# Four of the sixteen low halves of each two-stream norm move from VectorE to GpSimd

## What is computed

```python
def rms_norm(x, g):
    xf = x.astype(jnp.float32)
    y = xf * lax.rsqrt(jnp.mean(xf * xf, axis=-1, keepdims=True) + RMS_EPS)
    return (y * g.astype(jnp.float32)).astype(x.dtype)

def modulate(h, shift, scale):
    return h * (1.0 + scale) + shift

def sandwich_ffn(x, w_gate_up, w_down, g_pre, g_post, shift, scale, gate):
    h = modulate(rms_norm(x, g_pre), shift, scale)
    return x + 0.5 * gate * rms_norm(swiglu(h, w_gate_up, w_down), g_post)
...
    for l in range(DEPTH):
        last = l == DEPTH - 1
        mx = [m[:, None, :] for m in mod_vectors(c, w_mod[l], b_mod[l])]
        mc = mod_vectors(c_ctx, w_mod[l], b_mod[l])
```

## Time and profile before

| | before |
|---|---|
| median of 3 runs | 3280.05 us (3278.34 to 3292.75) |
| profiled execution, own time | 3276.89 us |
| its span | 3274.9 us |
| PE busy | 3064.8 us, 94% |
| DVE busy | 1678.6 us, 51% |
| ACT busy | 1354.5 us, 41% |
| POOL busy | 213.9 us, 7% |
| granted TensorE clock, mean | 0.960 of full speed |

### The profile page before, as it was taken

One profiled execution on the slowest core, in us unless ns is written; L12 is line 12 of the kernel. 1 busy time (PEld: TensorE's weight loads), 2 busy tenths in 40 slices (PEclk: granted clock), 3 DMA queues, 4 the chain that ended last, 5 costly groups with the idle time before them and its releaser, 6 DMA issues. The chain is left out here.

```text
span 3274.9 us, 52918 instructions
## 1 busy us (share of the span) xinstructions
PE 3064.8 (94%) x21712; PEld 2694.9 (82%) x21712; DVE 1678.6 (51%) x2574; ACT 1354.5 (41%) x2092; POOL 213.9 (7%) x304
## 2 busy tenths in 40 slices
PE   6999989989999899997989899998999999988998
PEld 4777858657777688876789889998799989988998
DVE  3332254552322633235655557656675677556765
ACT  3222232632222432223455455546464555454644
POOL 1111014101110000011200000000000000000000
PEclk9999989989999899998989999999899999989999
DMA  8555344135554223253245543554265546543553
GB/s 275 167 179 171 99 133 124 40 104 179 177 167 145 90 90 102 91 163 117 67 146 191 167 154 112 185 168 137 65 193 193 160 146 202 191 141 104 168 193 104
DMA packets 405772, 474.85 MB, mean 145 GB/s; under 512 B 10860, under 2 KB 383164, under 8 KB 405578
## 3 DMA queue, kind: packets, MB, share of 16 engines
q1 hardware_dynamic: 380176, 389.05, 36.9%
q0 software_dynamic: 24544, 82.74, 8.0%
q10 hardware_dynamic: 858, 0.29, 0.0%
HBM read 470.84 MB, written 4.84 MB: 145 GB/s over the span
## 5 line engine op out<-in xcount | busy, mean ns | idle before, releaser
L425 DVE TENSOR_TENSOR w_lo<-w_raw,w_hi 128x1024 fp32r<-128x1024 f32 x734 | 897.3, 1228 | 1268.8 <-ACT w_hi L422 1267.7
L433 PE MATMUL bank<-a_hi,w_hi 128*128 128x256 f32 (+1 forms) x3864 | 1241.3, 321 | 57.8 <-DVE a_lo L1398 16.6
L434 PE MATMUL bank<-a_lo,w_hi 128*128 128x256 f32 (+1 forms) x3864 | 1227.1, 318 | 0.0
L435 PE MATMUL bank<-a_hi,w_lo 128*128 128x256 f32 (+1 forms) x3864 | 1226.3, 317 | 0.0
L422 ACT ACTIVATE w_hi<-w_raw 128x1024 fp32r<-128x1024 f32 x734 | 771.1, 1056 | 987.5 <-PE bank L435 957.1
L433 PEld LDWEIGHTS bank<-a_hi,w_hi 128*128 128x128 f32 x3864 | 741.2, 192 | 134.5 <-issue 76.0
L435 PEld LDWEIGHTS bank<-a_hi,w_lo 128*128 128x128 f32 x3864 | 741.5, 192 | 50.5
L434 PEld LDWEIGHTS bank<-a_lo,w_hi 128*128 128x128 f32 x3864 | 741.4, 192 | 47.7
L433 PE MATMUL bank<-h_hi,w_hi 128*128 128x256 f32 (+1 forms) x1728 | 544.5, 315 | 0.0
L435 PE MATMUL bank<-h_hi,w_lo 128*128 128x256 f32 (+1 forms) x1728 | 539.6, 312 | 0.0
L434 PE MATMUL bank<-h_lo,w_hi 128*128 128x256 f32 (+1 forms) x1728 | 539.5, 312 | 0.0
(11 more groups left out here) (289 smaller groups left out, 2320.7 us busy)
## 6 DMA issues: line engine op xcount, KB each, us to landing
w_raw<-in_mlp_w SPq DMA_DIRECT2D x128, 1024.0 KB, 5.3
w_raw<-in_w_ffn_gate_up SPq DMA_DIRECT2D x88, 1024.0 KB, 5.3
m_raw<-in_w_mod POOLq DMA_DIRECT2D x128, 512.0 KB, 4.8
w_raw<-in_w_ffn_down SPq DMA_DIRECT2D x32, 1024.0 KB, 5.9
w_raw<-in_gla_w_in SPq DMA_DIRECT2D x24, 1024.0 KB, 5.5
w_raw<-in_w_in SPq DMA_DIRECT2D x16, 1024.0 KB, 6.0
w_raw<-in_ple_w_gate SPq DMA_DIRECT2D x16, 1024.0 KB, 5.1
w_raw<-in_w_ffn_down SPq DMA_DIRECT2D x16, 768.0 KB, 6.2
```

The source lines that it names most:

```text
L425: e.tensor_tensor(lo, raw, hi.bitcast(F32), ALU.subtract).then_inc(S.lo_ready.sem, 1)
L433: e.matmul(dst, hi, rhs_hi, start=start, stop=False)
L434: e.matmul(dst, hi, rhs_lo, start=False, stop=False)
L435: return e.matmul(dst, lo, rhs_hi, start=False, stop=stop)
```

## The change

In the five norms over both streams, piece 1 of every four (1, 5, 9 and 13 of 16: stream 1 of k0, k2, k4 and k6) gets its `a_lo` from GpSimd. DVE has one operation for it; GpSimd has two: it adds the shift (a column, broadcast) to `z` in place, and subtracts `a_hi` into `a_lo`. TensorE waits for GpSimd's count as well ahead of these blocks. `a_shared` stays as it is until the next norm, so that later products with a `ready` list wait for a count long reached.

```diff
@@ slot_products
                         if k0 + k in ready:
                             e.wait_ge(ready[k0 + k][0].sem, ready[k0 + k][1])
+                        if k0 + k in at.a_shared:
+                            e.wait_ge(S.pool.sem, at.a_shared[k0 + k])
@@ pre_norm
-                scaled, done = {}, {}
+                scaled, done, at.a_shared = {}, {}, {}
...
                     if j >= lag:
                         k, s, c = tiles[j - lag]
+                        if n == TT and (j - lag) % 4 == 1:
+                            if pool:
+                                e.wait_ge(S.act.sem, scaled[j - lag])
+                                e.tensor_tensor(z[:, k, c], z[:, k, c], shift[:, k, s:s + 1].to_broadcast([P, T]), ALU.add).then_inc(S.pool.sem, 1)
+                                e.wait_ge(S.pool.sem, S.pool.n + 1)
+                                e.tensor_tensor(a_lo[:, k, c], z[:, k, c], a_hi[:, k, c].bitcast(F32), ALU.subtract).then_inc(S.pool.sem, 1)
+                            S.pool.n += 2
+                            at.a_shared[k] = S.pool.n
+                            continue
```

More of the change, by code:

```diff
@@ L84, in __init__ @@
         self.a_order = None
+        self.a_shared = {}
         self.x_ready = None
```

## The result

| | before | with the change |
|---|---|---|
| median (6 runs each) | 3284.36 us | 3309.57 us |
| lowest to highest | 3278.34 to 3292.75 | 3299.47 to 3318.81 |
| profiled execution, span | 3274.9 us | 3303.8 us |

The ratio is 1.0075, with a 95% interval of 1.0047 to 1.0102: slower by 25 us (15 to 33). The forecast was slower, 3315 us, in a range of 3304 to 3325. The median of the kernel before is 3284.36 us over these six runs, where the forecast had started from 3280.05.

What follows compares the result with a forecast made beforehand. TensorE was taken as the bound, with VectorE counting only at norm heads. Terms 15.9 + 17.4 + 0.4 + 0.4 + 1.6 = 35.7 us on the profiled 3276.9 gave 3312.6, so a median about 3315; range 3304 to 3325.

Steps and rivals of the forecast that it cites:

- The large term: Norms 1 and 3: m_raw loads issued only after GpSimd's last pair, first product 7.3 us later; +15.9 and +17.4 us.
- rival 2: All five norms: loads exposed but engines not holding each other off, GpSimd ends at 10.4 us; +26.8 us, 3307; chance 0.12.
- norm 1: TensorE's first product there moves from 51.97 to 67.9 us, waiting for late m_raw loads: +15.9 us.
- norm 3: TensorE's first product there moves from 697.22 to 714.6 us, waiting for late m_raw loads: +17.4 us.
- first slot behind norm 3: TensorE's first products after that norm: 12.1 us before, at pace with VectorE; nothing added for clock or pace.
- norms 2 and 4: TensorE starts when GpSimd's block 0 pair is done, 3.25 us after first z instead of 2.84: +0.4 us each.
- norm 5: TensorE keeps pace with VectorE; its last block starts about 14.4 us after first z instead of 12.76: +1.6 us.
- I walked a norm by these durations, with the one that comes first holding the other off: Within a norm: VectorE stands still 3.2 us; GpSimd ends 13.0 and VectorE 14.3 us after first z.
- Landings: m_raw loads in norms 1 and 3: 5.3 us from the second load's issue to its landing.
- Rival 3: Worse: 7.3 us landings, lower clock for longer, GpSimd operations costing VectorE 0.6 us each; +44 us, 3324; chance 0.11.
- Code loading: GpSimd's first call after a code load pays about 6 us; if inside norm 1, last pair 1 to 2 us later, 3317.

Runs made afterwards that it cites:

- the probe: Kernel before plus two GpSimd scratch operations for each of pieces 1, 5, 9, 13: subtractions norm 2, copies norm 4, memsets norm 5; ran once, only timelines read.

## Why the prediction came out as it did

**The mechanism was right.** The large term, the loads of `m_raw` behind the pairs, is shown by three kernels that part it from everything else: without it no loss (0.9994), with it alone the whole loss (1.0075), with one pair of four ahead of them 1.0044. The time, 3309.6 us, lies inside the range, 5 us under the forecast. That flatters the sum: the kernel before came out 4.3 us above the median from which the forecast started, and the loss itself was 25 us (15 to 33), for 35.7 forecast. Of these 35.7 us the profile shows 29.0, nearer to the 26.8 of rival 2 (no hold) than to the forecast:

| term | forecast, us | measured, us | where the difference is |
|---|---|---|---|
| norm 1 | +15.9 | 18.26 - 4.41 = +13.9 | last pair 11.3 after the first z for 13.0; 6.95 from there to the product for 7.3 |
| norm 3 | +17.4 | 17.81 - 2.94 = +14.9 | 11.3 for 13.0; 6.5 for 7.3 |
| first slot behind norm 3 | 0 | 11.7 - 12.1 = -0.4 | no longer at VectorE's pace |
| norms 2 and 4 | +0.4 each | +0.5 each | |
| norm 5 | +1.6 | 12.50 - 12.76 = -0.3 | VectorE ends at 12.4, not 14.3 |

The two profiles differ by 28.9 us in span; of that 1.4 us lies ahead of the first norm (the first z at 48.94 against 47.56), and has nothing to do with the change. So 27.5 us are left for the 29.0 of the table, within what single executions scatter.

In the first slot behind norm 3 I had added nothing for the granted clock either. It did fall: 0.72 of full speed in TensorE's first 2.30 us and 0.95 over the slot, where it was 1.00 before. What that cost was less than what TensorE gained by finding all blocks ready.

**The step that was mis-sized** is "I walked a norm by these durations, with the one that comes first holding the other off", which let GpSimd hold a_lo for the whole of its recorded 0.64 or 0.73 us. That gave VectorE 3.2 us of standing still in a norm; it was 12.4 - 11.1 = 1.3 us. By the same walk GpSimd's last pair was to end 13.0 us after the first z and ended at 11.3, which is 1.7 us too much in each of norms 1 and 3. The hold is 0.51 us for a subtraction in the probe. In the changed kernel the a_lo of 55.69, met by an addition begun at 55.61, took 0.81 us, so it was let in 0.41 us after GpSimd had begun. The trace of before had the number, and I did not look at it: of the line with two inputs in SBUF at 563.94,

```profile
L1244 DVE TENSOR_TENSOR bias<-bias,na_mask_s x4: 2276/2746/2830, 563.9 to 1595.6; 128x2048 f32<-128x2048 f32 x4
```

the longest is 0.55 us over the shortest (both are in the pair of 563.94, where GpSimd's subtraction ran), and w_lo's 1655 is 0.44 over its 1218. I had read these rows for whether the engines hold each other, and taken for how long from GpSimd's duration. The Trainium skill ("SBUF — State Buffer", "SBUF: two separate sides") calls it a lock for the whole instruction. That led the same way, and measured by GpSimd's recorded times it does not hold here: VectorE is let in after 0.51 of 0.80 us. Either GpSimd lets go before it is done, or its recorded end lies behind its real one; which of the two it is, these runs do not show.

**Landings** were 5.2 and 4.7 us for the later of the pair, where I took 5.3 from the earlier trace rows. Rival 3's 7.3 us did not come, nor its longer stay at the lower clock: the clock over the first slot was 0.91 in norm 1, as before, and 0.95 in norm 3.

**Norms 2 and 4** went as forecast, TensorE released by GpSimd (+0.5 us for +0.4). **Norm 5** went the other way in sign, by 0.3 us: without the longer hold VectorE keeps a little of what was taken off it.

**Code loading** cost nothing that shows here: in the changed kernel the load instruction ran at 24.9 us, with 25.7 us of waiting behind it up to the first addition. With the loads of `m_raw` ahead of the pairs it ran at 43.5 us, and the first addition started at 49.32, 1.57 us after the first z (1.51 in norm 3), and took 0.61 us. The Trainium skill ("GPSIMD Engine Reference", "Instruction dispatch") puts the first call after such a load at about 6 us more; in both kernels GpSimd was idle for about that long or longer, so these runs can't tell.

## What to carry to other kernels

An engine that issues DMAs is a queue first. Before work is given to an idle one, look at which loads stand behind it in program order and who waits for them: GpSimd was 7% busy, and eight operations in front of two loads, done 11.3 us after the norm's start with their waits, cost 14 to 15 us each time. Issue such loads ahead of the work, and then look for the next ones behind it. When two engines share a path, read how long one is held from the victim's own spread (longest less shortest on one line), not from the other's duration.

## What the runs showed that the prediction did not have

- GpSimd holds VectorE's two-input operation for less than GpSimd's own recorded time, and by kind: 0.51 us of 0.80 for a subtraction, 0.15 to 0.20 us of 0.44 for a copy, none for a memset. VectorE's z, with one input in PSUM, was not held by any.
- With both engines at work, VectorE loses most of what it is spared: 1.6 us of operations less, 0.3 us earlier.
- The loads of the second slot stand behind the pairs too, and show once the first ones are moved: waits of 0.15 and 0.78 us in norm 3.
